# Second layer's attention: the weights are turned by a diagonal of gate over sum, made by GpSimd, in place of the identity

## The reference

```
gates = sigmoid(gate_logit)                  # one for each token, head and branch (3 branches)
s_c = q . kc * scale ; p_c = masked_softmax(s_c)      # compressed keys, 31 of them
o_c = p_c @ vc
s_s = q . k_sel * scale ; p_s = masked_softmax(s_s)   # selected blocks: with 512 tokens, all of them
o_s = p_s @ v_sel
s_w = q . k_win * scale ; p_w = masked_softmax(s_w)   # window of 512: all earlier tokens
o_w = p_w @ v_win
out = gates[0] * o_c + gates[1] * o_s + gates[2] * o_w
```

## Time and profile before

| what | value |
| --- | --- |
| median of 3 runs | 2304.69 us (2303.46 to 2310.64) |
| the profiled execution's own time | 2309.42 us |
| its span, first to last instruction | 2308.1 us |
| TensorE busy | 2234.1 us, 97% |
| VectorE busy | 1384.6 us, 60% |
| ScalarE busy | 554.4 us, 24% |
| GpSimd busy | 64.3 us, 3% |
| the stage of the change, first logits to last values | about 889 to 1062 us |

### The profile page before, as it was taken

One profiled execution on the slowest core, in us unless ns is written; L12 is line 12 of the kernel. 1 busy time (PEld: TensorE's weight loads), 2 busy tenths in 40 slices (PEclk: granted clock), 3 DMA queues, 4 the chain that ended last, 5 costly groups with the idle time before them and its releaser, 6 DMA issues.

```text
span 2308.1 us, 29724 instructions
## 1 busy us (share of the span) xinstructions
PE 2234.1 (97%) x11070; PEld 1625.1 (70%) x11070; DVE 1384.6 (60%) x3555; ACT 554.4 (24%) x1405; POOL 64.3 (3%) x79
## 2 busy tenths in 40 slices
PE   7999999999999999999999999999999999999987
PEld 6785678888888886557888888888767633333333
DVE  6696667666565648997765656767776422222224
ACT  2202342100010114774210100233563111111110
POOL 0000000000000000000000000000010011111000
PEclk9998999999999999999999999999999999999999
DMA  5221112222222321001222222222104899999997
GB/s 208 73 75 33 36 56 87 80 89 92 91 83 83 131 73 37 1 1 39 90 92 88 80 89 92 92 92 74 55 19 188 318 419 422 425 423 423 424 425 309
DMA packets 60208, 346.56 MB, mean 150 GB/s; under 512 B 9248, under 2 KB 10144, under 8 KB 42208
## 3 DMA queue, kind: packets, MB, share of 16 engines
q1 hardware_dynamic: 55360, 335.03, 38.1%
q0 software_dynamic: 3840, 6.46, 0.7%
q10 hardware_dynamic: 864, 3.15, 0.3%
HBM read 337.59 MB, written 17.30 MB: 154 GB/s over the span
## 4 chain that ended last, share of the span: by engine, by line
PE 73%; DMA 7%; DVE 5%; issue 1%; ACT 1%; SPq 0%; DVEq 0%; POOLq 0%
PE bank L613 26%; PE bank L619 7%; PE bank L626 7%; PE bank L634 7%; DMA places<-in_experts 7%; PE bank L2846 6%; PE bank L2854 3%; PE bank L602 2%; PE bank L2806 1%; PE bank L1007 1%; PE bank L992 1%; DVE exps L2077 1%; PE bank L1019 1%; PE bank L2819 1%; PE bank L1214 1%
## 5 line engine op out<-in xcount | busy, mean ns | idle before, releaser
L2846 PE MATMUL bank<-places,xT 128*64 128x512 f32 x824 | 183.9, 594 | 14.0 <-DMA places<-in_experts 13.9
L3053 DVE TENSOR_SCALAR square<-bank,mt 128x256 f32<-128x256 f32 x32 | 15.5, 484 | 287.0 <-ACT rope L2958 287.0
L2846 PEld LDWEIGHTS bank<-places,xT 128*64 128x64 f32 x824 | 59.4, 137 | 132.8 <-issue 118.1
L613 PE MATMUL bank<-u,ring 128*128 128x256 f32 x552 | 131.5, 381 | 1.1 <-DVE y_ab L1831 1.1
L1797 DVE TENSOR_TENSOR third<-first,bank 128x256 f32<-128x256 f32 x106 | 44.5, 420 | 146.7 <-PE bank L613 146.0
L1463 ACT ACTIVATE exps<-exps,small 128x128 f32<-128x128 f32 (+1 forms) x192 | 106.6, 560 | 79.0 <-DVE small L2077 78.4
L613 PE MATMUL bank<-h_sums,w_sum 128*128 128x256 f32 x512 | 121.0, 380 | 0.0
L613 PE MATMUL bank<-h,ring 128*128 128x256 f32 x512 | 121.0, 380 | 0.0
L613 PEld LDWEIGHTS bank<-u,ring 128*128 128x128 f32 x552 | 104.1, 191 | 17.4 <-issue 2.8
L613 PE MATMUL bank<-u_mlp_sums,w_sum 128*128 128x256 f32 x480 | 113.4, 380 | 0.0
L613 PE MATMUL bank<-u_mlp,ring 128*128 128x256 f32 x480 | 113.4, 380 | 0.0
(11 more groups left out here) (519 smaller groups left out, 4329.2 us busy)
## 6 DMA issues: line engine op xcount, KB each, us to landing
places<-in_experts SPq DMA_DIRECT2D x56, 2048.0 KB, 35.5
ring<-in_dense SPq DMA_DIRECT2D x216, 512.0 KB, 4.2
places<-in_experts SPq DMA_DIRECT2D x40, 1024.0 KB, 23.8
x<-in_experts SPq DMA_DIRECT2D x12, 1024.0 KB, 37.3
w<-in_experts SPq DMA_DIRECT2D x10, 1024.0 KB, 31.4
consts<-in_experts SPq DMA_DIRECT2D x10, 1024.0 KB, 32.2
x<-in_experts SPq DMA_DIRECT2D x4, 2048.0 KB, 32.3
consts<-in_consts SPq DMA_DIRECT2D x1, 2310.5 KB, 16.9
```

What stands on the lines that cost most here:

```text
L613: ins = pe.matmul(bank, w[:, j, :], x(j), start=j == 0, stop=j == 3)
L2846: ins = k.pe.matmul(bank[a * CAP:(a + 1) * CAP, :], xT[:, kk % 4, kk // 4, :], w[:, (2 * (kk % 2) + a) * EH:(2 * (kk % 2) + a + 1) * EH], ...
```

## The change

VectorE no longer scales the weights. It takes only the reciprocals (`dve_nsa_totals`) and signals `c_inverse`. A new queue of work on GpSimd (`pool_nsa`) makes for each item and head a matrix of 128x128: the identity times the column of reciprocals times the column of gates. It lies in one of eight tiles (`gate_diag`), used in turn; from the fifth item on GpSimd first waits until the turn of four items earlier has been done. `c_scaled` now counts these diagonals. TensorE turns the unscaled weights by a product with the diagonal, e transposed times diagonal, which turns and scales at once. That is a matmul in the usual mode, in place of the transpose instruction.

```diff
@@ buffers
+        k.diag = sb("gate_diag", [P, 8, P], stack=st)
@@ program
         vector_program(k)
+        pool_nsa(k)
         pool_sb(k)
@@ pe_nsa_turn
         pe.wait_ge(s["c_scaled"], 2 * n + a + 1)
-        e = sized_tile(k, n, b, a)
+        e, d = sized_tile(k, n, b, a), k.diag[:, (2 * n + a) % 8, :]
         for j in range(b + 1):
-            ins = pe.transpose(k.bank[4 + a][:, j * P:(j + 1) * P], e[:, j * P:(j + 1) * P], k.const("ident"))
+            ins = pe.matmul(k.bank[4 + a][:, j * P:(j + 1) * P], e[:, j * P:(j + 1) * P], d, start=True, stop=True)
@@ dve_nsa
         if 0 <= step - 2 < len(NSA):
-            dve_nsa_scale(k, step - 2)
+            dve_nsa_totals(k, step - 2)
@@
-def dve_nsa_scale(k, n):
+def dve_nsa_totals(k, n):
-    dve, s, own = k.dve, k.s, k.dve_own
-    m, x, b = NSA[n]
+    dve, s = k.dve, k.s
     neg, total, inv = soft_columns(k, n)
     dve.wait_ge(s["c_exp_done"], 2 * n + 2)
-    dve.wait_ge(own.sem, own.link(dve.reciprocal(inv, total)))
-    for a in range(2):
-        e, q = sized_tile(k, n, b, a), 6 * m + 3 * a + 1 + x
-        dve.tensor_scalar(e, e, inv[:, a:a + 1], k.gt[:, b, q:q + 1], ALU.mult, ALU.mult).then_inc(s["c_scaled"], 1)
+    dve.reciprocal(inv, total).then_inc(s["c_inverse"], 1)
@@
+def pool_nsa(k):
+
+    pool, s = k.pool, k.s
+    for n, (m, x, b) in enumerate(NSA):
+        neg, total, inv = soft_columns(k, n)
+        pool.wait_ge(s["c_inverse"], n + 1)
+        for a in range(2):
+            q = 6 * m + 3 * a + 1 + x
+            if n >= 4:
+                pool.wait_ge(s["c_t_done"], 2 * (n - 4) + a + 1)
+            pool.tensor_scalar(k.diag[:, (2 * n + a) % 8, :], k.const("ident"), inv[:, a:a + 1], k.gt[:, b, q:q + 1],
+                               ALU.mult, ALU.mult).then_inc(s["c_scaled"], 1)
```

More of the change, by code:

```diff
@@ L300, in signals @@
     s.new("lg_done", "masked", "exp_done", "t_done", "turned0", "turned1")
-    s.new("c_lg_done", "c_masked", "c_exp_done", "c_scaled", "c_t_done", "c_turned0", "c_turned1", "c_weighed")
+    s.new("c_lg_done", "c_masked", "c_exp_done", "c_inverse", "c_scaled", "c_t_done", "c_turned0", "c_turned1", "c_weighed")
     s.new("gates_exp", "cmp_k_in", "cmp_v_in", "cmp_2_in")
```

## The result

The changed kernel took 2335.1 us (2329.3 to 2338.6, 4 runs), the kernel before 2305.4 us in the same job. The ratio is 1.0123, with a 95% interval of 1.0095 to 1.0150: slower by some 28 us. The forecast was 2330.4 us, 25.7 us more than before, in a range of 2322 to 2343 us.

A forecast was written before the change was run, and what follows sets the result against it. TensorE, 97% busy, was taken as the engine to beat: 35.8 us of second records less 10.1 us of removed waits gives +25.7 us on 2304.7, so 2330.4 us, in a range of 2322 to 2343 us.

The forecast's parts named there:

- TensorE's own work: Second layer's attention: of each 21.1 us period, 2.0 us are TensorE's waits, 19.1 us its own work.
- A second record for each block: The turn: each of 320 transposes becomes a float32 matmul with one more record of 0.112 us, 35.8 us extra.
- The skill's rule: The turn: float32 transposes four times faster than matmuls, so three more records a block, 107 us extra; chance 0.03.
- The wait left at the compressed branch: Turn behind the compressed branch: TensorE still waits 0.71 us for the first diagonal, in place of 1.11.
- The waits that go: TensorE's waits in the attention: 10.1 us removed in all, including 0.60 us in each of 8 periods.
- GpSimd hidden but for one place: Diagonals on GpSimd: 0.46 us each, 7.4 us a period, no bound by the sum; a wait of 0.7 once a period.
- Rival B: Diagonals on GpSimd: the late link at 0.95 us or more each, +38.6 us, 2343 us; chance 0.12.
- Rival C: The turn: a matmul no dearer than the transpose, only waits change, -10.1 us, 2294.6 us; chance 0.04.
- Sum: Whole kernel: 35.8 us of extra records less 10.1 us of removed waits, +25.7 us.

The follow-up runs named there:

- e3: The changed kernel with VectorE's reciprocals ahead of the compressed branch's first part; period 23.89 us, ratio 1.0109 to the kernel before.
- e10: e1 with VectorE's scaling ahead of the compressed branch's first part; period 23.89 us, one run of 2327.7 us.
- e1: The kernel before with matmuls with the identity in place of transposes, VectorE still scaling, GpSimd idle; period 24.46 us, ratio 1.0117.
- e6: The changed kernel with the diagonals made by VectorE, GpSimd idle; period 24.33 us, ratio 1.0107 to the kernel before.
- e2: The changed kernel with transposes put back, diagonals still made and waited for, weights left without gate over sum; period 20.88 us, ratio 0.9990.
- e9: e2 with VectorE's reciprocals ahead of the compressed branch's first part; period 19.67 us, one run of 2294.4 us.
- e7: The changed kernel with each diagonal written twice by GpSimd; period 25.52 us, ratio 1.0154 to the kernel before.
- e5: The kernel before, transposes kept, GpSimd scaling the second head's weights, VectorE the first's, scaling ahead of the compressed branch's first part; period 19.67 us, ratio 0.9963.

## Why the prediction was right, point by point

- **TensorE's own work, 19.1 us of the 21.1.** Right. e3 and e10 give 23.89 us with matmuls and no wait. Less the extra of 4.8 (below) this is 19.1.
- **A second record for each block, 0.112 us, 35.8 in all.** Right in kind (640 records for 320), 7% short in size. The three turns above give 0.113 to 0.125, by 40 blocks a period 4.8 us and not 4.5, or 38.4 us in the stage. That is 2.6 us more than I had. I took the step between records inside a long run. The short turns have more beside it: four blocks cost 0.50 and not 0.45.
- **The skill's rule.** The Trainium skill's factor of four for float32 transposes ("TensorE: Matmul & The Clock Gate", section Terms) would have made it 107 us. Eight blocks took 0.93 us as transposes and 1.89 as matmuls: the factor is two.
- **The wait left at the compressed branch, 0.71.** Measured 0.64: the diagonal took 0.44 for my 0.46, and TensorE came 0.05 later.
- **The waits that go, 10.1 us.** They went, and a little more: 38.4 less the stage's 26.9 leaves 11.5 us. But the prediction put them beside VectorE's loss of work, and e1 shows the same waits gone with VectorE's work all there. The longer turns covered them. So the number held and its reason was half wrong: the relief itself, in this kernel, was worth nothing to be measured (24.49 and 24.46).
- **GpSimd hidden but for one place.** Right at the cost that it has (e6: 0.16 us a period). Two diagonals beside the rope took 1.24 us for 0.88, and no turn waited. With transposes (e2, e9) GpSimd isn't hidden.
- **Rival B's price.** For 0.95 us a diagonal it had +38.6, and e7 with some 0.9 has +38.0 in the stage. That is luck in part: B kept all the old waits and set 1.5 us at the one place, while in e7 that place has 1.07, other turns pay for a late second head, and 3.4 us come with a slow clock at the start.
- **Rival C, the other side.** The matmul is dearer, so it fell. Its price was wrong as well: with transposes I gave it -10.1 us, and e2 has -2.2. The step that failed was to keep 0.71 us for the wait at the compressed branch, which holds only if TensorE comes 0.45 later; with short turns it is 1.15, and the turns of two blocks wait for their second diagonal, 0.29 us twice in a period.
- **Sum.** Forecast +25.7. The records cost 2.6 us more than I had and the waits gave 1.4 more, so two small errors cancel in part. Seven periods of +3.37 are 23.6, the first steps and the last turns 3.3, together the stage's 26.9. The medians differ by 29.7, the ratio gives 28; what lies beyond 26.9 is no more than runs scatter.

## What to carry to other kernels

An operation folded into a neighbouring matmul was not free here, because that neighbour was a transpose and not a matmul. Each float32 transpose that became a float32 matmul left two records for one, and on the busiest engine that hides only in the engine's own waits; count the records of both kinds in the trace before choosing. When two engines are both near full, relief of the one is worth only the waits that it causes the other; find these one by one, for a single place in the order of the queue may hold most of them. If work must leave VectorE, let it go to an idle engine without passing through the bound one (e5).

## What the runs showed of the hardware that I had not expected

- GpSimd's `tensor_scalar` with two columns as scalars isn't slow: 0.44 us for 128x128 float32, and 1.05 for 128x512 in e5, where I had guessed 1.7. In e5 VectorE's own scaling always runs beside it; what it takes alone, no run shows.
- The same 128x512 took 1.56 us at 943.00 in e5, while VectorE began to rotate the queries with an operation of two SBUF inputs. So it was in all seven periods with such a rotation; in the eighth, which has none, it took 1.04 (1041.37). VectorE's operation:

```profile
943.39 0.69 DVE L1995 TENSOR_TENSOR rope<-y_c,consts 128x512 f32<-128x512 f32 x1
```

  The masks, one of whose inputs is a bank, ran beside diagonals at no cost that a row shows: the mask at 964.04 in the changed kernel took its usual 0.42, the diagonals 0.44 each. By the Trainium skill, "SBUF — State Buffer", section on two separate sides, both are the work of the lock on the port that VectorE and GpSimd share. The trace agrees that GpSimd is held up. It can't tell whether the port goes to whichever starts first, as that section says: GpSimd's record at 943.00 starts 0.39 before the rope's, which kept its 0.69, but 0.07 behind VectorE's scaling.
- A turn by matmuls made the group behind it shorter: the rope's two records took 1.02 us from their start to the next group behind transposes (937.78 to 938.80 in e2), and 0.96 behind matmuls (976.60 to 977.56 in the changed kernel). Why, no run here tells.
